# Two of twelve modulation tiles, and the product for the state matrix B, moved out of the first stage of a two-block network on one core

## What is computed

```
for layer in (0, 1):                       # attention, then S5
    mod   = silu(cond) @ ada_w[layer] + ada_b[layer]     # cond: c for the latent, c_ctx for the context
    shift, scale, gate = split(mod, 3)                   # 1024 columns each
    h     = x * (1 + scale) + shift
    y     = mixer(h @ w_in[layer]) @ w_out[layer]
    x     = layer_norm(alpha * x + gate * y)
# S5: bbar = ((abar - 1) / lam) * B, with abar = exp(lam * dt); state matrices of 128 groups
```

## Time and profile before

| | |
|---|---|
| median of 3 runs | 1649.02 us (1647.22 to 1656.89) |
| the profiled execution | 1654.81 us, span of its trace 1652.1 us |
| TensorE busy | 1541.9 us, 93% of the span |
| VectorE, ScalarE, GpSimd busy | 968.4, 794.0, 639.1 us |
| granted TensorE clock, mean | 0.968 |
| stage 1, modulation | 0 to 83.4 us |
| stage 2, projection | 83.4 to 312 us |
| stage 3, attention | 314 to 453 us |

### The profile page before, as it was taken

One profiled execution on the slowest core, in us unless ns is written; L12 is line 12 of the kernel. 1 busy time (PEld: TensorE's weight loads), 2 busy tenths in 40 slices (PEclk: granted clock), 3 DMA queues, 4 the chain that ended last, 5 costly groups with the idle time before them and its releaser, 6 DMA issues. The chain is left out here.

```text
span 1652.1 us, 28466 instructions
## 1 busy us (share of the span) xinstructions
PE 1541.9 (93%) x11474; PEld 1319.5 (80%) x11474; DVE 968.4 (59%) x1344; ACT 794.0 (48%) x1070; POOL 639.1 (39%) x497
## 2 busy tenths in 40 slices
PE   4899999899889899999979999989999999999998
PEld 0478888678778688888869987779999877789997
DVE  6354432188654618757937555755766665457665
ACT  2332212356432467878564435635545364464552
POOL 0069997299789690738912005111000100210000
PEclk9789999999989999999979999989999999999999
DMA  9977775366453576998866445325454333254541
GB/s 387 427 289 250 235 249 203 127 189 198 139 199 110 199 240 197 256 278 256 213 200 257 176 186 218 123 82 186 198 214 167 127 142 128 102 227 176 208 159 44
DMA packets 119290, 328.81 MB, mean 199 GB/s; under 512 B 33396, under 2 KB 72692, under 8 KB 102920
## 3 DMA queue, kind: packets, MB, share of 16 engines
q1 hardware_dynamic: 116310, 301.71, 52.7%
q10 hardware_dynamic: 2868, 25.54, 4.4%
HBM read 282.17 MB, written 36.65 MB: 193 GB/s over the span
## 5 line engine op out<-in xcount | busy, mean ns | idle before, releaser
L3144 PE MATMUL ffn_ps<-ffn_x_lead,w_lead 128*128 128x256 f32 x672 | 188.3, 280 | 1.1 <-DVE w_rest L3223 1.1
L3144 PE MATMUL ffn_ps<-ffn_x_lead,w_rest 128*128 128x256 f32 x672 | 188.6, 281 | 0.0
L3144 PE MATMUL ffn_ps<-ffn_x_rest,w_lead 128*128 128x256 f32 x672 | 188.4, 280 | 0.0
L401 POOL TENSOR_TENSOR w_rest<-resident_ring,w_lead 128x2048 fp32r<-128x2048 f32 x7 | 32.1, 4592 | 387.7 <-ACT w_lead L397 200.1
L3223 DVE TENSOR_TENSOR w_rest<-resident_ring,w_lead 128x2048 fp32r<-128x2048 f32 x42 | 96.1, 2292 | 83.7 <-ACT w_lead L3188 83.7
L365 PE MATMUL qkvz_ps<-qkvz_w_lead,h_lead 128*128 128x512 f32 x320 | 125.7, 393 | 3.0 <-POOL h_rest L662 3.0
L3144 PEld LDWEIGHTS ffn_ps<-ffn_x_lead,w_lead 128*128 128x128 f32 x672 | 126.1, 188 | 2.1 <-issue 1.4
L3144 PEld LDWEIGHTS ffn_ps<-ffn_x_rest,w_lead 128*128 128x128 f32 x672 | 126.4, 188 | 0.7
L3144 PEld LDWEIGHTS ffn_ps<-ffn_x_lead,w_rest 128*128 128x128 f32 x672 | 126.3, 188 | 0.0
L365 PE MATMUL qkvz_ps<-qkvz_w_rest,h_lead 128*128 128x512 f32 x320 | 125.4, 392 | 0.0
L365 PE MATMUL qkvz_ps<-qkvz_w_lead,h_rest 128*128 128x512 f32 x320 | 125.3, 392 | 0.0
(11 more groups left out here) (547 smaller groups left out, 4458.1 us busy)
## 6 DMA issues: line engine op xcount, KB each, us to landing
resident_ring<-in_ffn_gu SPq DMA_DIRECT2D x22, 2048.0 KB, 9.0
ffn_wd<-in_ffn_down SPq DMA_DIRECT2D x22, 1024.0 KB, 4.9
resident_ring<-in_ada_w SPq DMA_DIRECT2D x8, 2048.0 KB, 12.7
xc<-s_q_scratch SPq DMA_DIRECT2D x128, 128.0 KB, 3.4
resident_x<-in_s_bT SPq DMA_DIRECT2D x64, 256.0 KB, 3.8
resident_ring<-in_attn_w_in ACTq DMA_DIRECT2D x8, 2048.0 KB, 10.1
s_W_scratch<-resident_x SPq DMA_DIRECT2D x64, 256.0 KB, 2.9
resident_ring<-in_s_w SPq DMA_DIRECT2D x32, 512.0 KB, 6.4
```

Source lines behind the costliest of these rows:

```text
L401: self.core.nc.gpsimd.tensor_tensor(self.slots[1][0], self._raw(r), self.slots[0][0].bitcast(F32), ALU.subtract).then_inc(self.rest_made, 1)
L3144: last = nc.tensor.matmul(ps[s][f][:, m, :], w_part[w][m][:, k, f * P:(f + 1) * P], x_part[x][:, k, :], start=(k, w, x) == (0, 0, 0), stop ...
```

## The change

**Stage 1** has 10 tiles; the gate tiles of layer 1 (entries 10 and 11) go to the end of the order and are not loaded here. `gates` has only layer 0's row, stored behind the last tile's issue. The first tile goes to `third`. The seven table banks stand behind three tiles and no longer behind four. B is not loaded or multiplied here; only the small factor `scale` is stored (128 KB).

**Stage 2**: a new class `ScaledInput` loads B and `scale` to rows of `z` (SP, behind the first four blocks of `InputWeights`), VectorE multiplies a quarter of B in each of groups 0 to 3, between the weight's rests and the rotation, and ScalarE issues the store of 2048 KB. The loads that were the first two tiles of `w_out0` are the two gate tiles. In `ModulatedParts` VectorE makes the value of block 0 ahead of the first weight rest and ahead of the lead, and ScalarE makes the values of blocks 4 and 6.

**Stage 3**: ScalarE issues four small loads more (condition, `pick`, bias twice) and a Silu; TensorE multiplies the two gate tiles in step -1 and sums them; ScalarE copies the sums and then issues the two loads of `w_out0`; VectorE adds the bias; ScalarE stores the gates, which lie in a part of `pT[1]`, and VectorE waits for that store before it writes `pT[1]` in step 1.

**S5 mixer**: one block more is turned ahead of the first product, and block 0's value goes ahead of the first rest.

```diff
-ADA_ORDER = (4, 5, 10, 11, 6, 7, 8, 9, 0, 1, 2, 3)
-ADA_GATES = 4
+ADA_ORDER = (4, 5, 6, 7, 8, 9, 0, 1, 2, 3, 10, 11)
+ADA_LATE = 2
+ADA_GATES = 2
-ADA_TABS = {5: (0, 1), 6: (2, 3), 7: (4, 5), 8: (6,)}
+ADA_TABS = {5: (0, 1, 2), 6: (3, 4, 5), 7: (6,)}
+ADA_SLOT = (2, 0, 1)
...
                 for s in range(2):
                     sp.wait_ge(mm_done, NT - 2 + s)
                     core.load(sp, s, d["attn_w_in"][s])
                     if s == 0:
                         tab_q_store(sp)
+                        sp.wait_ge(biased, 1)
+                        sp.dma_start(d["mod"][0], gates[:]).then_inc(stored, 16)
                 tab_stores(sp)
                 sp.wait_ge(stored, 16)
...
     def leads(self, act, ks):
         for k in ks:
+            if k == 0:
+                act.wait_ge(self.value_made, 1)
             act.wait_ge(self.turned, k + 1)
...
+            if self._scalar_value(k):
+                for r, cols in self.HALVES:
+                    last = self.core.nc.scalar.activation(self.temps[k // 2][:, cols], self.banks[k % self.nb][:, cols], ACT.Identity, bias=self._modT(k, r),
+                                                          scale=scale(k, r))
...
-                    core.load(act, s, d["attn_w_in"][g + 2] if g < NT - 2 else d["w_out0"][g + 2 - NT])
+                    core.load(act, s, d["attn_w_in"][g + 2] if g < NT - 2 else d["ada_w"][len(ADA_ORDER) - ADA_LATE + g + 2 - NT])
...
                 act.wait_ge(core.q_stored, 16)
+                scaled.store(act)
...
                 def rotate(g, s, dst, between=None):
                     split.ahead_vector(dve, g, s)
+                    if between is not None:
+                        between(dve, g)
...
+                    if i < 0:
+                        for m in range(ADA_LATE):
+                            modulation_tile(m)
+                        pick_sums(0)
...
+                act.dma_start(ccT[:], d["cc"]).then_inc(cond_in, 16)
+                act.dma_start(pick[:], d["pick"]).then_inc(cond_in, 16)
+                for r in range(2):
+                    act.dma_start(gate_bias[r:r + 1], d["ada_bg"][1:2]).then_inc(cond_in, 16)
...
+                act.wait_ge(cond_in, 64)
+                act.wait_ge(zeroed, 1)
+                nc.scalar.activation(sT[:, :, 0:2], ccT[:], ACT.Silu).then_inc(cond_ready, 1)
+                queries(1)
+                keep_sums(0)
+                exponentials(0)
+                keep_sums(1)
+                for m in range(ADA_LATE):
+                    act.wait_ge(tile_done, m + 1)
+                    core.load(act, m, d["w_out0"][m])
+                for i in range(0, NH + 2):
                     step(i, i % 2)
+                    if i == 0:
+                        act.wait_ge(gate_made, ADA_LATE)
+                        act.dma_start(d["mod"][1], gates).then_inc(gates_stored, 16)
...
+                    if i < 1:
+                        add_bias(i + 1)
+                    if i == 1:
+                        dve.wait_ge(gates_stored, 16)
                     if exists(i):
                         for b in (1, 2):
                             dve.wait_ge(p_turned, i * 3 + 2 + b)
...
+class ScaledInput:
+    CHUNKS = 4
...
+    def loads(self, sp):
+        sp.wait_ge(self.core.tables_stored, 48)
+        sp.dma_start(self.b, self.core.d["s5_bA"]).then_inc(self.b_in, 16)
+        sp.dma_start(self.scale, self.core.d["s5_scale"]).then_inc(self.scale_in, 16)
...
+        self.chain.run(v.tensor_tensor(self.swapped, by(1), b[:, ::-1], ALU.mult))
+        self.chain.run(v.tensor_tensor(b, by(0), b, ALU.mult))
+        v.tensor_tensor(b[:, 0], b[:, 0], self.swapped[:, 0], ALU.subtract)
+        last = v.tensor_tensor(b[:, 1], b[:, 1], self.swapped[:, 1], ALU.add)
...
-                            if k == KT - mod.nb:
-                                mod.transposes(pe, range(mod.nb, KT))
+                            if k == 2:
+                                mod.transposes(pe, range(mod.nb + 1, KT))
```

More of the change, by code:

```diff
@@ L646, in values @@
         for k in ks:
+            if self._scalar_value(k):
+                continue
             bank = self.banks[k % self.nb]
-            dve.wait_ge(self.lead_made, k + 1)
+            if k:
+                dve.wait_ge(self.lead_made, k + 1)
+            else:
+                dve.wait_ge(self.turned, 1)
             for r, cols in self.HALVES:
@@ L688, in _ @@
                 weights.begin(sp)
+                scaled.loads(sp)
                 for n in range(W_QKVZ):
@@ L738, in _ @@
                 chain = Chain(dve, steps)
+                mod.values(dve, range(0, 1))
                 split.rest(dve, 0, 0, 0, 0)
-                mod.values(dve, range(0, HK))
+                mod.values(dve, range(1, HK))
                 split.rest(dve, 0, 0, 0, 1)
@@ L759, in rotate @@
                         nc.vector.tensor_tensor(dst(t), straight[:, t, :], crossed[:, t, :], ALU.add).then_inc(dve_free, 1)
-                with chain.loop(2, 4) as i:
-                    for s in range(2):
-                        rotate(i * 2 + s, s, lambda t: q[:, t, bass.ts(i * 2 + s, NW)])
+                for g in range(4):
+                    rotate(g, g % 2, lambda t: q[:, t, g * NW:(g + 1) * NW], scaled.make)
                 dve.wait_ge(core.q_stored, 16)
@@ L810, in attention @@
         ident = core.ident
+        ccT, sT, pick = ph.sb("ccT", [P, KT, 2]), ph.sb("sT", [P, KT, 32]), ph.sb("pick", [P, 2])
+        sums_kept = [pT[i][:, 0, :] for i in range(ADA_LATE)]
+        gate_bias, gates = [pT[i][0:2, 1:3, :].rearrange("r l n -> r (l n)") for i in range(2)]
+        gate_bank = [ps_p[2][0:2, :], ps_y[0:2].rearrange("r t n -> r (t n)")]
+        names = "cond_in zeroed cond_ready tile_done sums_ready picked gate_made gates_stored".split()
+        cond_in, zeroed, cond_ready, tile_done, sums_ready, picked, gate_made, gates_stored = [ph.sem(n) for n in names]
+        tile_landed = [16 * (core.used[s] + 1) for s in range(ADA_LATE)]
+        for s in range(ADA_LATE):
+            core.used[s] += 1
         spare = ph.sb("spare", [P, DM])
@@ L891, in _, with modulation_tile, pick_sums @@
                 prime(pe, yz_turned, 1)
+                def modulation_tile(i):
+                    pe.wait_ge(cond_ready, 1)
+                    pe.wait_ge(core.landed[i], tile_landed[i])
+                    for turn in range(2):
+                        for j in range(4):
+                            last = nc.tensor.matmul(ps_p[i][32 * j:32 * j + 32, :], sT[:, 4 * turn + j, :], core.tile(i)[:, 4 * turn + j, :],
+                                                    start=turn == 0, stop=turn == 1)
+                    last.then_inc(tile_done, 1)
+                def pick_sums(i):
+                    pe.wait_ge(sums_ready, i + 1)
+                    nc.tensor.matmul(gate_bank[i], pick[:], sums_kept[i], start=True, stop=True).then_inc(picked, 1)
                 turn_queries(0)
@@ L1272, in empty_on_scalar @@
         if n == 4:
-            nc.scalar.activation(scale[:], banks[0][:, 0:2, :], ACT.Copy)
+            nc.scalar.activation(scale, banks[0][:, 0:2, :], ACT.Copy)
             level(1, banks[0][:, 2:4, :]).then_inc(emptied, 1)
@@ L2070, in scan @@
                         dve.sem_inc(scanned, 1)
+                mod.values(dve, range(0, 1))
                 rest(0)
-                mod.values(dve, range(KT))
+                mod.values(dve, range(1, KT))
                 for n in range(STEPS):
```

119 lines of the change are left out of this document (74 added, 45 removed).

## The result

The changed kernel takes 1645.31 us (median of 10 runs, 1636.23 to 1649.95); the kernel before, measured beside it, 1649.64 (10 runs, 1646.6 to 1656.89). The ratio is 0.9948 with a 95% interval of 0.9928 to 0.9967: about 0.5% faster, 5 to 12 us, and inside the 1% that I called no change. The forecast was 1639.6, with a range of 1631 to 1647. The profiled execution took 1649.23 (before: 1654.81).

A forecast was written before the change was run, and what follows sets the result against it. Stage 1 was taken as bound by DMA bytes, nearly everything behind it by TensorE. Terms -14.2 (stage 1), -1.2 (projection), +6.8 (attention), -0.8 (mixer) sum to -9.4; on 1649.0 that gives 1639.6 us, range 1631 to 1647.

The forecast's parts named there:

- Stage 1, -14.2: Stage 1: three loads fewer; SP's store of the gates and TensorE end it almost together, 14.2 us sooner.
- my 69.2: Stage 1: predicted end at 69.2 us, when SP's store of the gates has landed and the barrier is passed.
- the rival with a chance of 0.14: Stage 1: table banks in a row and lower clock keep TensorE until 75; -8 us, total 1645.8; chance 0.14.
- B's 4.9 us: Stage 1: time counted for B's load of 2048 KB at 427 GB/s, saved by moving B away.
- Projection, -1.2: Projection: block 0's value made first brings blocks 1 to 3 earlier, B's quarters cost 0; 1.2 us saved.
- my threshold of 8.6: Projection: a quarter of B on VectorE, put at 4.2 us, costs time only from 8.6 us on.
- Attention, +6.8: Attention, step 1: VectorE's copies to `pT` wait for the gates' store queued behind both `w_out0` loads; 6.8 us lost.
- First scores, -0.6: Attention start: gate products fill TensorE's pause, so the second scores run at the upper clock and end 0.6 us sooner.
- the rival of 0.12: Attention: starts at the lower clock, its first products later and idling longer; +3 us, total 1642.6; chance 0.12.
- Mixer, -0.8: S5 mixer: the same reordering and two values moved from VectorE to ScalarE save 0.8 us, between 0 and 1.
- The first rival (the store doesn't wait): Attention: the gates' store doesn't wait for the `w_out0` loads; -0.6 there, total 1632.2 us; chance 0.18.

The follow-up runs named there:

- bearly: The changed kernel with matrix B loaded, multiplied and stored in stage 1 as before the change, none of it in the projection: 1649.76 us, ratio 0.9983.
- bite: The changed kernel with both `w_out0` loads issued right ahead of the store of the gates, after ScalarE's step 0: 1651.38 us in one execution.
- again: The changed kernel, unedited, measured and traced a second time: 1644.14 us, ratio 0.9929.

## Why the prediction was right, and where not

The time fell into the range, faster by less than 1%; of the 9.4 us forecast the first measurement gives 4.3 by the medians and 8.6 by the ratio.

- **Stage 1, -14.2.** Right as a mechanism: the store of the gates behind `s_q_scratch` on SP's queue ends it, in all seven executions with these tables (TensorE idle 1.3 to 3.9 us). What I had wrong is that I took SP and TensorE for two ends side by side. SP's issue waits for a tile that TensorE multiplies, so a TensorE that the lower clock makes late moves SP's store too. The mean of the seven is 70.6, 1.4 above my 69.2, and three of them ended at 72.1 to 73.2: in these the rival with a chance of 0.14 (banks in a row and the lower clock) came in, at 73 rather than 75. Of B's 4.9 us bearly shows 4.1 for its bytes; VectorE's products with it, which my sum did not have, then ended the stage 0.9 later.
- **Projection, -1.2.** The first product came 1.1 earlier, B's quarters cost nothing, and behind its first blocks TensorE waited for no rest. The total varies by 2.6 us with the clock behind the start (228.7 to 231.2), more than the term: whether the 1.1 us reach the end of the stage is not shown. A quarter took longer than I said: the second one's rows (2.31, 1.65, 1.10 and 1.78) make 6.8 us, not 4.2, still under my threshold of 8.6.

```profile
133.46 2.31 DVE L1481 TENSOR_TENSOR z<-z 128x1024 f32<-128x1024 f32 x1
135.81 1.65 DVE L1482 TENSOR_TENSOR z<-z 128x1024 f32<-128x1024 f32 x1
137.49 1.10 DVE L1483 TENSOR_TENSOR z<-z 128x512 f32<-128x512 f32 x1
138.52 1.78 DVE L1484 TENSOR_TENSOR z<-z 128x512 f32<-128x512 f32 x1
```

- **Attention, +6.8.** This is the step that failed: VectorE's 6.8 us of waiting for the store behind the two loads, with "ScalarE issues both loads of `w_out0` at about 330.4 (head 0's exponentials end at 329.5, the copy of the sums 0.6 later)" as its start. The wait was 0.41 us in the first execution and 0 in the second. The size came out near (4.6 and 6.1 us longer), the reason did not: that the time fell into the range owes something to luck. The wait vanished from both sides. In the changed kernel the loads left at 320.17, when TensorE had done the gate tiles, while the exponentials and the copy written ahead of them in ScalarE's program ran until 322.8 and 323.3; so VectorE came to its copies 14.7 us after the loads' issue, not 11.5. And the store landed 15.1 us after it (13.9 in the second execution), where I had 18.2. What took the time instead is two things. I looked for who waits on ScalarE's queue and left out who shares the DMA engines with it: SP's queue, which feeds GpSimd. GpSimd and its last store had 3 to 4 us to spare in the attention, and the loads took 7 to 10; they ended the stage in the second execution. TensorE's own end came 4.5 and 2.8 us later, by the first scores and by the lower clock, and ended the stage in the first. GpSimd's end was a rival that I didn't have.
- **First scores, -0.6.** They were at the lower clock, the rival of 0.12; TensorE's second scores at the upper, as forecast. The issues ahead of K's copies made the pause: with them ahead the first scores came 5.8 us after the stage's first product in the mean of eight executions, with them behind 4.2 in that of four. With them ahead the first scores ran at the lower clock in seven of the eight (3.43 to 3.75 us), with them behind in one of the four; that the pause brings the lower clock is likely by this count, and not shown.
- **Mixer, -0.8.** Too small: about 2 (24.67, 24.68 and 23.38 against 21.8 to 22.3 in nine executions of eleven).
- **The first rival (the store doesn't wait).** What it said of VectorE came true (0.41 us of waiting, then 0), what it said of the store did not (it landed 15.1 us after the loads' issue, and 12.3 after its own in bite), nor did its time of 1632: removing the wait leaves the other bounds.

## What to carry to other kernels

When a big load moves to another stage, look at what small transfers share the DMA engines with it on any queue, and how much slack their consumer has in that stage, not only at what is queued behind it. Cut it into pieces that the other stream's buffers can outlast, and put them where that stream has room. And where a stage leaves the DMA bound, the work that stood in its pauses (here table banks) must fit the pauses that are left, at the lower clock too.

## What was not expected of the hardware

- ScalarE's DMA issues left 2.6 us before the activation written ahead of them had begun (320.17 against 322.73): only the semaphores that the issue waits for held it.
- 4 MB in two loads on one queue made 128 KB loads on the other take 11.8 us in place of 3.3 (again, and the attention of the kernel before); the same bytes in pieces of 512 KB, one each 7.4 us, made GpSimd wait for nothing.
- Beside GpSimd a product of 512 elements on VectorE took 0.68 to 1.78 us, one of 1024 1.53 to 2.31 (1.22 without GpSimd beside it, and in stage 1 of bearly with the same matrix).
- Stretches of the same code behind the mixer's start differed by up to 8.9 us between eleven executions (1090.4 to 1099.3), with a granted clock of 0.962 to 0.973 over the whole.
